# A hybrid block pair on one core: the opening read, summed and multiplied in two halves of features

## The reference, cut to what matters

```python
c_act = jax.nn.silu(c)
mod = c_act @ w_ada[l] + b_ada[l]                      # 1024 x 6144, six parts of 1024
sh1, sc1, g1, sh2, sc2, g2 = [m[:, None, :] for m in jnp.split(mod, 6, axis=-1)]
h = _standardize(x) * (1.0 + sc1) + sh1
mix = _hybrid_mixer(h, w_in[l], ...)                   # h @ w_in, then mLSTM heads and an S5 state space
x = _layer_norm(ALPHA * x + (1.0 + g1) * mix, ...)
```

## Time and profile before

| | |
|---|---|
| median of 3 runs | 1578.58 us (1578.58 to 1580.55) |
| profiled execution, its time | 1578.71 us |
| its span on the core | 1576.6 us |
| PE busy | 1555.4 us (99%), 7406 products |
| DVE, ACT, POOL busy | 751.9, 628.1, 681.7 us |
| PE on the chain that ended last | 80% |

### The profile page before, as it was taken

The page is one execution under the profiler, slowest core; times in us unless marked ns, Lnnn a source line. Parts: engine busy times, 40 slices in busy tenths (PEclk is TensorE's granted clock), DMA queues, the critical chain, the costliest instruction groups (busy, mean ns, idle before and its releaser), DMA issues.

```text
span 1576.6 us, 18787 instructions
## 1 busy us (share of the span) xinstructions
PE 1555.4 (99%) x7406; PEld 1260.4 (80%) x7406; DVE 751.9 (48%) x1295; ACT 628.1 (40%) x1135; POOL 681.7 (43%) x520
## 2 busy tenths in 40 slices
PE   9999999999999999999999999999999999999998
PEld 6888867788888888888888887568878888888886
DVE  6999524646666352133307698863432420022103
ACT  3534563543435333233332434673442542234322
POOL 1575333244554544454454454024413544444442
PEclk7999999999999999999999999999999999999999
DMA  8676532278534353333333442003213333333331
GB/s 319 138 110 155 134 101 80 55 234 277 197 107 135 114 168 125 100 94 94 107 108 99 136 120 81 14 28 94 81 40 94 104 97 97 103 90 98 96 105 67
DMA packets 223296, 181.08 MB, mean 115 GB/s; under 512 B 24284, under 2 KB 185948, under 8 KB 223080
## 3 DMA queue, kind: packets, MB, share of 16 engines
q1 hardware_dynamic: 214080, 166.68, 36.7%
q10 hardware_dynamic: 9128, 13.19, 2.5%
HBM read 173.28 MB, written 6.56 MB: 114 GB/s over the span
## 4 chain that ended last, share of the span: by engine, by line
PE 80%; ACT 1%; DVE 1%; POOL 0%; issue 0%; DVEq 0%; ACTq 0%
PE banks L649 13%; PE banks L650 13%; PE banks L655 13%; PE banks L731 9%; PE banks L732 9%; PE banks L736 9%; PE banks L778 3%; PE banks L761 1%; PE banks L762 1%; PE banks L763 1%; PE banks L1097 1%; PE banks L1110 1%; PE banks L1197 1%; PE banks L985 1%; PE banks L1183 0%; PE banks L1184 0%
## 5 line engine op out<-in xcount | busy, mean ns | idle before, releaser
L2570 POOL TENSOR_TENSOR w_lo<-raw,w_hi 128x512 fp32r<-128x512 f32 (+1 forms) x484 | 646.4, 1359 | 788.4 <-ACT w_hi L1267 787.5
L1267 ACT ACTIVATE w_hi<-raw 128x512 fp32r<-128x512 f32 (+1 forms) x484 | 275.9, 619 | 324.2 <-PE banks L736 244.4
L649 PE MATMUL banks<-h_hi,w_hi 128*128 128x512 f32 x936 | 367.2, 392 | 0.0
L650 PE MATMUL banks<-h_lo,w_hi 128*128 128x512 f32 x936 | 364.3, 389 | 0.0
L655 PE MATMUL banks<-h_hi,w_lo 128*128 128x512 f32 x936 | 250.2, 389 | 0.0
L649 PEld LDWEIGHTS banks<-h_hi,w_hi 128*128 128x128 f32 x936 | 175.7, 188 | 38.3 <-issue 1.7
L650 PEld LDWEIGHTS banks<-h_lo,w_hi 128*128 128x128 f32 x936 | 175.8, 188 | 36.6 <-issue 0.7
L655 PEld LDWEIGHTS banks<-h_hi,w_lo 128*128 128x128 f32 x936 | 175.7, 188 | 36.6
L2388 DVE SCALAR_TENSOR_TENSOR banks<-att_area,cols,banks 128x512 f32<-128x512 f32 x116 | 87.5, 754 | 3.4
L731 PE MATMUL banks<-w_hi,u_hi 128*128 128x512 f32 x224 | 87.1, 389 | 0.0
L732 PE MATMUL banks<-w_hi,u_lo 128*128 128x512 f32 x224 | 87.1, 389 | 0.0
(11 more groups left out here) (458 smaller groups left out, 2593.4 us busy)
## 6 DMA issues: line engine op xcount, KB each, us to landing
raw<-in_w_in SPq DMA_DIRECT2D x57, 512.0 KB, 4.3
raw<-in_w_ffn_up SPq DMA_DIRECT2D x44, 512.0 KB, 3.9
raw<-in_w_up SPq DMA_DIRECT2D x32, 512.0 KB, 4.0
raw<-in_w_down SPq DMA_DIRECT2D x32, 512.0 KB, 3.7
ada_ring<-in_w_ada SPq DMA_DIRECT2D x24, 512.0 KB, 5.7
raw<-in_w_ffn_down SPq DMA_DIRECT2D x20, 512.0 KB, 3.7
raw<-in_w_s_glu SPq DMA_DIRECT2D x16, 256.0 KB, 3.1
raw<-in_w_mlstm_down SPq DMA_DIRECT2D x8, 512.0 KB, 7.0
```

The lines of the kernel that those rows point to most:

```text
L649: te.matmul(ps, wv[0][:, i, :], rh, start=(i == 0), stop=False)
L650: te.matmul(ps, wv[0][:, i, :], rl, start=False, stop=False)
L1267: sc.activation(W_HI[SLOT[key]][:, part_], raw[:, RAW_SLOT[key], part_], ACT.Copy).then_inc(*hi_set.up((key, n_)))
L2570: gp_.tensor_tensor(W_LO[s_][:, part_], raw[:, RAW_SLOT[key], part_], W_HI[s_][:, part_].bitcast(F32), ALU.subtract).then_inc(*lo_made.up( ...
```

## The change

1. `w_ada` comes as 16 DMAs of 512 KB in place of nine: eight for features 0 to 511 (two blocks of rows, 512 columns of shift or of scale each), then us blocks 0 and 1, then eight for features 512 to 1023. SP no longer waits between them. The DVE tile now holds shift and scale of one half; DVE sums six blocks of the first half and all eight of the second.
2. A us block now holds 256 rows (two features) and all 512 columns. Four banks are summed at once: for each feature 8 products, for each pair of features 8 low products (`us_high`, `us_low`). All four us outputs are ready only after the last feature.
3. PE: three turned features at a time (banks 4, 5, 6), the sums in bank 7, keep_busy 8, 3, 2 in place of 8, 2, 2. ACT scales features 1 and 3 too. DVE puts the low parts of features 0 to 3 between the sums of the second half.
4. `s5_matrices` comes one block later in SP's order.
5. S5 work on PE, ACT and DVE moves by two blocks: {6, 8, 10, 15}. The outputs now come after om 7. SP's `ys_rows` DMAs stand ahead of gb 1, the `ysT` read ahead of gb 2, the kernel rows ahead of om 4. ACT runs `conv_out(4, 8)` after the gate copy, and `ys_gelu` together after `values_out(3)`. DVE takes the gate bias before `ysT`. POOL's toep memset comes two blocks later.

```diff
+        ada_place += [(1, 2 * i, part(buf, at, 2, D)) for i, (buf, at) in enumerate(((usys, 0), (usys, 2 * D), (s5a, 8704), (s5a, 8704 + 2 * D)))]
-        ADA_PE = ((1, 3), (1,))
+        ADA_PE = ((1, 3), ())
-        feature_blocks("us", w_in, OFF_US, US)
+        for m in range(KD // 2):
+            BLOCKS["us", m] = [(w_in[2 * m * P:2 * (m + 1) * P, OFF_US:OFF_US + US * P].rearrange("(k p) c -> p k c", p=P), 2, US * P)]
 # PE
+            def us_high(f):
+                m, i = divmod(f, 2)
+                ((w_hi, _),) = block(("us", m), False)
+                pe.wait_ge(*h1_lo[f])
+                if f < 5:
+                    turn_h1(f + 3)
+                pe.wait_ge(*hi_set[("us", m), i])
+                for b, ps in enumerate(us_banks):
+                    te.matmul(ps[:, :], w_hi[:, i, b * P:(b + 1) * P], h_hi[:, f, :], start=(f == 0), stop=False)
+                    te.matmul(ps[:, :], w_hi[:, i, b * P:(b + 1) * P], h_lo[:, f, :], start=False, stop=False)
...
             first_columns(0)
-            for f in range(4):
+            for f in range(3):
                 turn_h1(f)
+            keep_busy(3)
+            other_columns(0)
             keep_busy(2)
...
+            for f in range(KD):
+                us_high(f)
+                if f % 2:
+                    us_low(f // 2)
+                if f == 3:
+                    other_columns(1)
...
-            s5_after = {4: [s5_kernel], 6: [lambda: s5_turn(0), lambda: s5_turn(1)], 8: [s5_inputs], 13: [s5_outputs]}
+            s5_after = {6: [s5_kernel], 8: [lambda: s5_turn(0), lambda: s5_turn(1)], 10: [s5_inputs], 15: [s5_outputs]}
 # ACT
             for f in range(KD):
+                if f == KD // 2:
+                    high_to(3)
+                if f % 4 == 0:
+                    act.wait_ge(*mod_set["h1", f // 4, 1])
                 modulated("h1", f, mod[:, KD + f:KD + f + 1], mod[:, f:f + 1], h1_sv, h1_dv, h1_hi)
-                if f == 5:
-                    high_to(2)
+            high_to(4)
...
-                act.wait_ge(*gemm["us", m])
+                act.wait_ge(*gemm["us", KD // 2 - 1])
...
-            s5_after = {1: [s5_pads], 4: [s5_kernel], 6: [lambda: s5_turn(0), lambda: s5_turn(1), s5_tables], 10: [lambda: conv_out(0, 2)], 13: [s5_outputs], 14: [lambda: conv_out(2, 4)], 15: [lambda: conv_out(4, 8)]}
+            s5_after = {3: [s5_pads], 6: [s5_kernel], 8: [lambda: s5_turn(0), lambda: s5_turn(1), s5_tables], 12: [lambda: conv_out(0, 2)], 15: [s5_outputs, lambda: conv_out(2, 4)]}
...
             sc.dma_start(rows[32:32 + H1, 2, :], rows8[H1:2 * H1, :]).then_inc(*moved.up())
+            conv_out(4, 8)
...
             values_out(1)
-            ys_gelu(0)
             high_ahead("gb", 0)
-            ys_gelu(1)
+            gate_branch(0)
             values_out(2)
-            ys_gelu(2)
             values_out(3)
-            ys_gelu(3)
-            gate_branch(0)
+            high_ahead("gb", 1)
+            for J in range(US):
+                ys_gelu(J)
 # DVE
+            half_sums(0, ada_dve(0))
+            half_columns(0)
+            half_sums(1, (0,))
+            h1_low(0)
+            h1_low(1)
+            half_sums(1, (1, 2))
+            h1_low(2)
+            h1_low(3)
+            half_sums(1, (3, 4, 5, 6, 7))
+            half_columns(1)
 # SP
+            ada_half(0)
             for r_, (key, parts) in enumerate(STREAM):
-                if r_ == 0:
-                    sp.wait_ge(*ada_in[-3].all)
-                if r_ == NRAW:
+                if r_ == 2:
+                    ada_half(1)
+                if r_ == NRAW + 1:
                     s5_matrices()
-                if key == ("gb", 0):
+                if key == ("gb", 1):
                     sp.wait_ge(*y5_out.all)
```

More of the change, by code:

```diff
@@ L506, in build @@
         x_in = [signal(f"x{i}_in", 1, 16) for i in range(2)]
-        ada_in = [signal(f"ada{i}_in", 1, 16) for i in range(len(ada_place))]
+        ada_in = [signal(f"ada{i}_in", 2, 16) for i in range(len(ada_place))]
         ring_in = [signal(f"ada_ring{i}_in", ADA_ORDER[i::NADA], 16) for i in range(NADA)]
@@ L551, in build @@
         ada_step = signal("ada_step", [(p_, kk) for p_ in (3, 4, 2, 5) for kk in range(KD - 1)])
-        mod_set = signal("mod_set", [0, 1, 3, 4])
+        mod_set = signal("mod_set", [("h1", hf, q_) for hf in range(2) for q_ in range(2)] + [3, 4])
         g_set = signal("g_set", [(2, 0), (2, 1), (5, 0), (5, 1)])
@@ L693, in feature_pair @@
                         last.then_inc(*gemm.up(key))
[L695 to L715, removed]
         def token(key, kt, hi, lo, ready, free, banks=(0, 1, 2, 3), between=None):
@@ L845, in tensor @@
                 transpose(("c5", i), [c_nat[i][:, J, :, :].rearrange("p a b -> p (a b)") for J in range(4)], c_turned[2 * i + 1])
-            for m in range(2, US):
-                feature(("us", m), h_hi, h_lo, h1_ready, us_out[m])
             def s5_kernel():
@@ L2013, in vector, with half_sums, half_columns, h1_low @@
             dve.wait_ge(*c_set.all)
-            for p_ in range(2):
-                for kk in ada_dve(p_):
-                    n, rows_ = ada_rows_at[p_, kk]
-                    ada_add(p_, kk, rows_, ada_in[n].all)
-                    if (p_, kk) == (1, 6):
-                        ada_columns(0, 0, 0.0)
-            ada_columns(1, KD, 1.0)
-            dve.wait_ge(*mod_set[1])
-            for f in range(0, KD, 2):
+            def half_sums(hf, kks):
+                for kk in kks:
+                    n, rows_ = ada_rows_at[hf, kk]
+                    ada_add(hf, kk, rows_, ada_in[n].all)
+            def half_columns(hf):
+                dve.wait_ge(*ada_col[hf])
+                for q_ in range(2):
+                    at_ = q_ * KD + 4 * hf
+                    ve.scalar_tensor_tensor(mod[:, at_:at_ + 4], bank[7][:, KD * hf + 4 * q_:KD * hf + 4 * q_ + 4], float(q_), col("b_ada", at_, 4), ALU.add, ALU.add).then_inc(*mod_set.up(("h1", hf, q_)))
+            def h1_low(f):
+                low_part(h1_hi, f, h_lo[:, f, :], ps_of(("h1", f))[:, :], 1.0, h_hi[:, f, :], h1_lo)
+            half_sums(0, ada_dve(0))
[8 more added lines that the diff above has]
+            half_columns(1)
+            dve.wait_ge(*mod_set["h1", 1, 1])
+            for f in range(4, KD, 2):
                 modulated_low("h1", f, KD, 0, h1_dv, h1_hi, h1_lo)
@@ L2164, in vector @@
                 conv(f)
-            dve.wait_ge(*ys_in.all)
-            for J in range(US):
-                ve.scalar_tensor_tensor(ysT[:, J, :], usT[:, J, :], col("s5_d", J), ysT[:, J, :], ALU.mult, ALU.add).then_inc(*ys_raw.up(J))
             lo, hi = slice(0, H1), slice(32, 32 + H1)
@@ L2174, in vector @@
             ve.tensor_scalar(R(3, lo), rows8[lo, :], col("b_gate", 0, 1, 0, H1), None, ALU.add).then_inc(*dve.step())
+            dve.wait_ge(*ys_in.all)
+            for J in range(US):
+                ve.scalar_tensor_tensor(ysT[:, J, :], usT[:, J, :], col("s5_d", J), ysT[:, J, :], ALU.mult, ALU.add).then_inc(*ys_raw.up(J))
             for J in range(US):
@@ L2617, in sync, with ada_half @@
                 sy.dma_start(x_tok[:, 2 * i:2 * i + 2, :], io["x"][0, 2 * i * P:2 * (i + 1) * P].rearrange("(t p) d -> p t d", p=P)).then_inc(*x_in[i].up())
[L2618 to L2620 removed]
+            def ada_half(hf):
+                for n, (p_, k0, place_) in enumerate(ada_place):
+                    if p_ == hf:
+                        for q_ in range(2):
+                            src = io["w_ada"][0, k0 * P:(k0 + 2) * P, q_ * D + 512 * hf:q_ * D + 512 * (hf + 1)]
+                            sy.dma_start(place_[:, :, 512 * q_:512 * (q_ + 1)], src.rearrange("(k p) c -> p k c", p=P)).then_inc(*ada_in[n].up(q_))
+            ada_half(0)
             def qk_weights(h):
```

63 lines of the change are left out of this document (29 added, 34 removed).

## The result

The changed kernel took 1594.32 us (median; 1590.19 to 1595.84), the kernel before on the same chip 1578.96: a ratio of 1.0091, 95% interval 1.0070 to 1.0112, so 15.4 us slower by the medians. The profiled execution of the changed kernel took 1590.19 us (span 1588.0), 11.5 us more than that of before (1578.71), and it was the quickest of its four; the traces account for those 11.5, and what the others lost beyond them is taken up with e7. The forecast was 1583.9, between 1576.5 and 1589.0. The sign was right and the time lay outside the range.

What follows compares the result with a forecast made beforehand. The prediction took PE as the bound, with ACT's list deciding behind the S5 outputs. Its terms, -3.5 + 0.5 + 10.9 - 3.0 + 0.3 = +5.2 us on 1578.71, gave 1583.9 us, range 1576.5 to 1589.0.

Steps and rivals of the forecast that it cites:

- What bounds the kernel: From the first us product PE is the bound; behind the S5 outputs ACT's list is level with PE's.
- H - V: From values_out(0)'s start on ACT (V) to head_inputs(3)'s last record on PE (H): forecast put head_inputs(3) as far behind V as before.
- The first half of `w_ada`: Opening: halved DMAs cost nothing while PE's work covers them; first scale by ACT at 27.2, first us product near 29.
- From there to xm 0: Opening, from first scale at 27.2: DVE's sum just hidden, PE idle 43.8 to 46.2, xm 0 at about 60.0, -3.5 us.
- POOL: +0.5, between 0 and 2: S5 stretch: POOL's low parts, 6.9 us a block beside DVE's products, are slower than PE eats them: +0.5 us.
- Two blocks ahead of E: Two blocks now come before the last S5 output product ends on PE (E): +10.9 us.
- V - E: From the S5 outputs' end on PE (E) to values_out(0)'s start on ACT (V): 18.5 us, 3.0 less than before.
- The clock: PE's clock may fall in the wait for a bank behind the S5 outputs: +0.3 us.
- The S5 chain: DVE's preparation 8.5 us later; powers end at 109.6, PE turns them at 111.2: slack 1.6, cost nothing.
- A: Rival: PE never waits for ACT behind the S5 outputs and keeps the opening's gain: -3.0 us, 1575.7; chance 0.17.
- B: Rival: quick opening (xm 0 at 58.3) and quick landing of the weight block: 0.0, up to +3 us; chance 0.23.
- C: Rival: opening gives nothing, through low clock or POOL and S5 preparation stalling PE: +8.5 to +11 us; chance 0.12.

Runs made afterwards that it cites:

- e7: The changed kernel run once more, unaltered: 1591.03 us, ratio 1.0080.
- e10: Changed kernel with e8's ACT edits, S5 outputs back at 13, and POOL's low parts of us 2 and 3 only after DVE's second-half sums: 1577.17 us, ratio 0.9996.
- e3: Changed kernel with ACT making the high part of xm 1 ahead of the first us output and that of xm 2 behind it: 1585.08 us.
- e8: Changed kernel with the early high parts of e3, and exp and sin of S5 ahead of the high part of xm 0: 1583.61 us.
- e6: Changed kernel with eight of DVE's twelve large power products cut to two powers, so part of the computation is left out: 1589.23 us.
- e1: The kernel before with only part 5 of the change, the S5 work two blocks later and the new order: 1587.01 us, ratio 1.0049.
- e5: Changed kernel with part 5 taken back and the ACT edits of e8: 1580.31 us, ratio 1.0013.

## Why the prediction was right or wrong

**What bounds the kernel**: right. PE is the bound except where a list of another engine is level with it, and H - V = 33.3 to 33.6 in every kernel with the full computation confirms that ACT's list is level from V on.

**The first half of `w_ada`**: right, as far as its mark goes. The first us product came at 29.45, forecast 29. The window from 3 to 24 us moved 393 GB/s where it had been 409:

```profile
3.00:24.00 21.00, 19.80 (x64) 13.06 (x63) 13.73 (x28) 10.66 (x14) 1.83 (x2) 0.76 1.05 393
```

With the DMAs halved the rate was 4% lower, and PE's cover hid it. The Trainium skill ("DMA: Bandwidth & Descriptors", section "Bandwidth") asks for batches of at least 1 MiB. Here, with many DMAs in flight, the larger ones of before moved 409 GB/s and those of 512 KB 393.

**From there to xm 0**: the mechanism right, 1.3 us too optimistic (61.31, forecast 60.0). PE's first record behind the hole in the timeline is this one:

```profile
46.89 0.83 PE L756 MATMUL banks<-ident,s5a 128*128 128x128 f32 x4 [2.46 <-DVE h_lo L1804]
```

It was forecast for 46.2. The sums were put at 1.33 us each from a row in which POOL was idle; beside POOL they took 1.77 (e10, where POOL is held back, has 1.33 again), and so DVE's sum was not hidden but 0.4 us late. The rest is in the products after the hole, of which eight and not four ran at half the clock.

**POOL: +0.5, between 0 and 2: the step that failed.** It measured 6.9. The forecast took POOL's rate beside DVE rightly, 6.9 us a block against PE's 5.44, but asked only about the gap between xm 4 and xm 5. What counts at such rates is the lead that POOL has when the slow stretch begins. PE eats half a block in 2.72 us and POOL makes one in 3.2 to 3.5 as long as DVE's products last, 40 us; before, POOL entered that stretch with xm 1 done, after the change with xm 1 to do, and two halves at 3.24 are 6.5 us. The us outputs were counted only for when the first lets xm 0 start, and not for what stands behind all four in ACT's list: the high part of xm 1, POOL's lead, and by way of POOL the load of xm 5. e3 and e8, which alter nothing but the order on ACT, take 6.3 of the 6.9 away. POOL's rate alone doesn't make the loss: with POOL quicker, in e6, it was 6.2 by way of that load.

**Two blocks ahead of E**: +10.9 as forecast (E moved by 11.3 in e1, with a wait of 0.2 at the turns among it). **V - E**: forecast -3.0, measured -4.8 in the changed kernel and -2.7 in e1. The landing of the weight block at E + 13.3 was the uncertain row; it was E + 13.8 in e1 and E + 11.75 after, both within the bounds given. **The clock**: forecast +0.3, measured nothing; the turns took 3.58 us in place of 1.91, and PE's slack behind V took it.

**The S5 chain**: "cost nothing, slack 1.6" held. The powers ended at 106.87 (103.61 + 3.26), forecast 109.6, and e5 shows what the cover is worth: without the two blocks there is a wait of 3.2 us.

**The rivals.** A fell, as PE waited 4.2 to 6.5 us for ACT behind E in every kernel with the outputs at 15; B fell with POOL: of its opening (58.3) 61.3 was reached, of its landing (V = E + 15.3) E + 16.7, and the losses behind xm 0 took more than both gave. C is what happened, at its end: "POOL and the preparation of S5 stall PE by 2 us or more" was given +8.5 to +11 and a chance of 0.12. Its sign, xm 0 after 62, did not show (61.31), and neither did its low clock through four features (eight products); it came by POOL. Its price was read too low since its place, the order on ACT between us outputs and high parts, had not been looked at. Sum by the forecast's terms with what they measured: -2.2 + 6.9 + 10.9 - 4.8 + 0.0 = +10.8 for the profiled run's 11.5. The 3.9 us from there to the median were in no term.

## What to carry to other kernels

When work that used to be spread out (four outputs, one after the other) comes ready at once, list what stands behind it on the engine that takes it, and who feeds on that; here the bill came some 12 us later, on PE by way of POOL (and, had POOL been quick, by way of a load that waits for POOL), and was three times what the opening had won. For a producer that is slower than its consumer for a while, the price is set by the lead at the start of that stretch, so write down both rates, its length and the lead. And undo a change part by part: the order moved by two blocks cost 8.2 us, and the turns needed it but the outputs did not.

## What the runs showed of the hardware

POOL and DVE, each with two fp32 inputs in SBUF, ran nearly one instruction at a time: POOL's 128x512 difference took 1.27 us alone and 3.0 to 3.5 beside DVE's products of 2304 or 2048 elements; those of 2304 took 2.54 alone and 3.5 to 3.65 beside POOL, those of 2048 3.2 to 3.4 beside it. Four of DVE's 128x1024 sums took 5.32 alone, and 7.07 (in e3 8.19) with POOL beside them. Even the smallest can be caught, as the timeline of DVE in e3 shows: an operation on 16 elements took 1.13 us while POOL was busy, and 0.18 right after.

```profile
63.64 1.13 DVE L2084 TENSOR_TENSOR s5a<-s5a 128x16 f32<-128x16 f32 x1
64.81 0.18 DVE L2085 TENSOR_TENSOR s5a<-s5a,cols 128x16 f32<-128x16 f32 x1
```
